# Layer-norm statistics of a two-layer diffusion step: variance, root and reciprocal on 128x3 token columns

## Chip, cores and metric

The kernel runs on one core of a Trainium2 chip. The time is that of one execution on the device, in microseconds. A core has TensorE (PE in the rows; PEld is its loading of weights), VectorE (DVE), ScalarE (ACT), GpSimd (POOL) and SyncE (SP), which issues transfers. Each works through its own list of instructions in order and waits on semaphores for the others.

## The reference

One step of a two-layer network over 384 tokens (128 context, 256 latent) of width 1024: layer 0 has an mLSTM and attention mixer and a dense SwiGLU, layer 1 a bidirectional Mamba-2 mixer and top-2-of-8 experts. Each of the four sub-layers ends in a layer norm, and these four norms are what the change touches:

```python
def layer_norm(x, g, b):
    xf = x.astype(jnp.float32)
    mu = xf.mean(-1, keepdims=True)
    var = jnp.mean(jnp.square(xf - mu), -1, keepdims=True)
    return ((xf - mu) * lax.rsqrt(var + EPS) * g + b).astype(x.dtype)

def post_norm_layer(x, mods, mixer, channel, ln):
    sh1, sc1, g1, sh2, sc2, g2 = mods
    y, state = mixer(x * (1 + sc1) + sh1)
    x = layer_norm(ALPHA * x + g1 * y, ln[0], ln[1])
    x = layer_norm(ALPHA * x + g2 * channel(x * (1 + sc2) + sh2), ln[2], ln[3])
    return x, state
```

All inputs are float32. The values of a token's norm are one mean and one variance over the 1024 features, so 384 of each.

## The kernel before

Activations lie with the features on the partitions: `zT[:, b, :]` is block b (of KB = 8) of 128 features by T = 384 tokens. A mean over features is therefore a sum over partitions and blocks. TensorE makes it with the matrix `onesm` (128x128, every entry 1/1024) as one operand and a block as the other: the result, in PSUM bank 6, has the mean of each of the 384 tokens, the same on all 128 partitions. The same with `sqT`, the squares from ScalarE (L740), gives the mean square in bank 7. A float32 product is two passes in the trace, so a product appears as x2 and a group of three as x6.

The norms are numbered ln = 0 to 3. In norm 0 (after the mixer's output products `mixo`) and norm 2 (after `ssdo`) six of the eight blocks are first added up on GpSimd (L588, L591; `SUMMED`), and TensorE takes the sum in one go (`sums`), with block 6 before it and block 7 behind. In norm 1 all eight blocks are taken one by one, block b-1 behind the down products of block b. In norm 3, the last, blocks 4 and 5, the sum of four, and a pair added up on VectorE are taken at the end. `after_block` sets these places. There is no scheduler: what stands in each engine's function is its order.

When mean (bank 6) and mean square (bank 7) are complete, the engines go on in `deviation` (ScalarE) and `norm_steps` (VectorE):

- ScalarE squares the mean (L748) and copies it to SBUF (L749), which GpSimd waits for to centre blocks 4 to 7 (L600).
- VectorE takes the difference of mean square and squared mean (L1366) and centres blocks 0 and 1 (L1361).
- ScalarE takes the root into `stdr` (L751).
- VectorE takes the reciprocal (L1371) and multiplies block by block (L1377), with the centring of blocks 2 and 3 and the low parts (`low`, L1671 in norm 0, L1735 in norm 1) between.
- ScalarE applies the modulation (L759) and writes the rounded high part (L891, L944); VectorE subtracts it for the low part; TensorE starts the next stage (L2527 in norms 0 and 1, L2820 in norm 2) with block 0's.

All of L748 to L1371 work on 128x384, with the same row on all partitions. Semaphores: `mean_mm` and `var_mm` from TensorE, `sq_ready` and `std_ready` from ScalarE, `dev_ready` and `norm_ready` from VectorE, `ax_ready` from GpSimd. `gss` and `gsd` are two small tiles of 128x3 that layer 1's gated norm uses too (L1042, L1894). In norm 2, ScalarE splits the first tile of expert weights (L1130) between the root and the modulation.

Of the kernel before, what the change touches and what calls it, by code (L numbers as in the profile page):

```python
# [16 lines left out]
ALU = mybir.AluOpType  # L17
ACT = mybir.ActivationFunctionType
X = mybir.AxisListType.X

P = 128
D = 1024
KB = D // P
TP, TS = 128, 256
T = TP + TS
C = T // P
# [72 lines left out]
def build(nc, i, o):  # L99
    ctx = ExitStack()  # L100
    with ctx:
# [24 lines left out]
        uT = placed("uT", [P, KB, T])  # L126
        zT = placed("zT", [P, KB, T])
        sqT = placed("sqT", [P, KB, T])
# [3 lines left out]
        onesm = sb("onesm", [P, P])  # L132
# [4 lines left out]
        ps = ctx.enter_context(nc.psum_tensor("ps", [P, 8, 512], F32))  # L137

        ident = cons[:, CI["ident"][0]:CI["ident"][1]]
# [102 lines left out]
        epsc = sm.take(1)  # L242
        hsq = qkr.rearrange("p c n -> p (c n)")[:, 0:HA * C * HD].rearrange("p (h c d) -> p h c d", h=HA, c=C)
        knew_v = wa.take(P)
        stdr = placed("stdr", [P, T])
        mean2, var, meanr = (uT[:, b, :] for b in (7, 6, 5))
        dsums = [uT[:, b, :] for b in (4, 4, 4, 0)]
        zpair = uT[:, 1, :]
        masks = stdr[:, 0:2 * P].rearrange("p (e t) -> p e t", e=2)
# [59 lines left out]
        gss = sm.take(C)  # L309
        gsd = sm.take(C)  # L310
# [86 lines left out]
        def S(name):  # L397
            if name not in sems:
                sems[name] = ctx.enter_context(nc.semaphore(name))
            return sems[name]  # L400
# [334 lines left out]
        def _(act):  # L735
            step = Serial(act, S("act_step"))
# [8 lines left out]

            def deviation(ln):
                act.wait_ge(S("mean_mm"), 2 * ln + 2)
                nc.scalar.activation(mean2, ps[:, 6, 0:T], ACT.Square).then_inc(S("sq_ready"), 1)  # L748
                nc.scalar.activation(meanr, ps[:, 6, 0:T], ACT.Copy).then_inc(S("sq_ready"), 1)  # L749
                act.wait_ge(S("dev_ready"), DEV * ln + KB + 2)  # L750
                nc.scalar.activation(stdr[:, :], var, ACT.Sqrt, bias=epsc).then_inc(S("std_ready"), 1)  # L751

            def modulated(layer, half, ln, b):

# [478 lines left out]
        def _(v):  # L1233
            step = Serial(v, S("dve_step"))
            V = nc.vector
# [123 lines left out]
            def norm_steps(ln, low=None):  # L1359
                def center(b):  # L1360
                    V.tensor_tensor(zT[:, b, :], zT[:, b, :], ps[:, 6, 0:T], ALU.subtract) \  # L1361
                        .then_inc(S("dev_ready"), 1)

                v.wait_ge(S("var_mm"), ln + 1)
                v.wait_ge(S("sq_ready"), (KB + 2) * ln + KB + 1)
                V.tensor_tensor(var, ps[:, 7, 0:T], mean2, ALU.subtract).then_inc(S("dev_ready"), 1)  # L1366
                v.wait_ge(S("sq_ready"), (KB + 2) * (ln + 1))
                center(0)
                center(1)
                v.wait_ge(S("std_ready"), ln + 1)  # L1370
                step(V.reciprocal(stdr[:, :], stdr[:, :]))  # L1371
                for b in range(KB):
                    if b < MID:
                        v.wait_ge(S("dev_ready"), DEV * ln + KB + b + 3)
                    else:
                        v.wait_ge(S("ax_ready"), ax_count(ln, "centered", b - MID + 1))
                    V.tensor_tensor(zT[:, b, :], zT[:, b, :], stdr[:, :], ALU.mult).then_inc(S("norm_ready"), 1)  # L1377
                    if b + 2 < MID:
                        center(b + 2)
                    if low and b >= 2:  # L1380
                        low(b - 2)
                if low:
                    low(KB - 2)
                    low(KB - 1)
# [56 lines left out]
            for e in range(2):  # L1441
                running_max(e, 0, 0.0)
                first, second = (1, 2) if e == 0 else (2, 1)
# [761 lines left out]
        def _(pe):  # L2205
            M = nc.tensor
# [21 lines left out]
            def first_mean(ln):  # L2228
# [2 lines left out]
                M.matmul(ps[:, MEAN_BANK[ln], 0:T], onesm[:, :], zT[:, 0, :], start=True, stop=True) \  # L2231
                    .then_inc(S("mean_mm"), 1)

            def moments(ln, *blocks):

                for b in blocks:
                    first = b == (0 if SUMMED[ln] == 0 else SUMMED[3] if ln == 3 else KB - 2)
                    last = ln < 3 and b == KB - 1
                    pe.wait_ge(S("dev_ready"), DEV * ln + b + 2)
                    m = M.matmul(ps[:, 6, 0:T], onesm[:, :], zT[:, b, :], start=first, stop=last)  # L2240
                    if last:
                        m.then_inc(S("mean_mm"), 1)
                    pe.wait_ge(S("sq_ready"), (KB + 2) * ln + b + 1)
                    m = M.matmul(ps[:, 7, 0:T], onesm[:, :], sqT[:, b, :], start=first, stop=last)
                    if last:
                        m.then_inc(S("var_mm"), 1)

            def sums(ln):

                pe.wait_ge(S("ax_ready"), ax_count(ln, "summed", 1))  # L2250
                M.matmul(ps[:, 6, 0:T], onesm[:, :], dsums[ln], start=False, stop=False)
                M.matmul(ps[:, 7, 0:T], onesm[:, :], sqT[:, 0, :], start=False, stop=False)

            def after_block(ln, b, first):

                if b == first:
                    first_mean(ln)
                elif SUMMED[ln] and b == KB - 1:
                    moments(ln, KB - 2)
                    sums(ln)  # L2260
                    moments(ln, KB - 1)
                elif not SUMMED[ln] and b > first:
                    moments(ln, *(range(b) if b == first + 1 else (b - 1,)))
                    if b == KB - 1:
                        moments(ln, b)

            pe.wait_ge(S("cact_ready"), 1)
            for t in range(ADA_PE):
# [7 lines left out]
            for k in range(KB):  # L2276
                pe.wait_ge(S("u_ready"), k + 1)
                m = M.matmul(ps[0:32, 2, 0:T], w[:, k * 32:(k + 1) * 32], uT[:, k, :], start=k == 0, stop=k == KB - 1)
# [16 lines left out]
            for t in range(3):  # L2295
                for part in range(4):
                    proj(t, part)
                    if (t, part) == (0, 1):
                        pe.wait_ge(S("gates_moved"), 1)
                        for n in range(2):  # L2300
                            m = M.matmul(ps[:, 6 + n, 0:T], con("spread", 32)[:, n * P:(n + 1) * P], gates32,
                                         start=True, stop=True)
                        m.then_inc(S("gate_mm"), 1)
            for j in range(4):
# [6 lines left out]
                for k in range(KB):  # L2311
                    c0 = k * 256 + (j % 2) * P
                    m = M.matmul(ps[:, 3 + j % 2, 0:T], slot(g % RING)[:, c0:c0 + P], uT[:, k, :],
                                 start=k == 0, stop=k == KB - 1)
# [4 lines left out]
            for c in range(C):  # L2319
                for j in range(4):  # L2320
                    m = M.transpose(ps[:, c, j * P:(j + 1) * P], qkr[:, c, j * P:(j + 1) * P], ident)
                m.then_inc(S("qkT_mm"), 1)
            for c, at in ((0, 0), (1, 2), (2, 3)):
                m = M.transpose(ps[:, 5, at * P:(at + 1) * P], qkr[:, c, 512:640], ident)
# [52 lines left out]
            for n in range(12):  # L2377
                q, c = n // C, n % C
                src = gli if q == 0 else rows[:, q - 1, :]
                m = M.transpose(ps[:, 5 + n // 4, (n % 4) * P:(n % 4 + 1) * P], src[:, c * P:(c + 1) * P], ident)  # L2380
            m.then_inc(S("cols_mm"), 1)
            for c in range(C):
                for j in range(4):
                    m = M.transpose(ps[:, c, j * P:(j + 1) * P], tokk[:, c, j * P:(j + 1) * P], ident)
# [583 lines left out]
            moments(3, 4, 5)  # L2968
            sums(3)
            pe.wait_ge(S("b16_ready"), 2)  # L2970
            M.matmul(ps[:, 6, 0:T], onesm[:, :], zpair, start=False, stop=True).then_inc(S("mean_mm"), 1)
            pe.wait_ge(S("b16_ready"), 3)
            M.matmul(ps[:, 7, 0:T], onesm[:, :], sqT[:, KB - 2, :], start=False, stop=True).then_inc(S("var_mm"), 1)

# [119 lines left out]
```

## Time and profile before

| | |
|---|---|
| median of 3 runs | 1596.39 us |
| lowest, highest | 1595.52, 1599.64 us |
| the profiled execution's own time | 1599.93 us |
| its span, first to last instruction | 1598.2 us |
| TensorE busy, mean granted clock | 94%, 0.977 |
| VectorE, ScalarE, GpSimd busy | 79%, 50%, 21% |
| end of the sums in norms 0, 1, 2, 3 | 299.6, 603.7, 970.5, 1585.3 us |

All times in the rows are microseconds from the start of the span. The granted clock is a share of 2.4 GHz: 1.00 or 0.50 (1.2 GHz). Matmuls are pipelined: one's duration runs from its start to its last result, and the next starts earlier. So the distance from start to start is what a product costs in a series, and the duration counts only for the last one.

### The profile page before, as it was taken

Reading aid. Unit: us, or ns where it says so; the run is one execution under the profiler, and the core shown is the slowest. Engines: PE = TensorE matmul, PEld = TensorE weight load, DVE = VectorE, ACT = ScalarE, POOL = GpSimd, SP = SyncE. Lnnn points to the kernel's source line nnn. Section 1 sums busy time; section 2 is a strip of 40 time slices with the busy share of each in tenths; the row PEclk is TensorE's granted clock in tenths of the full one; section 3 lists DMA queues with packets and bytes.
Section 4 is the critical chain, followed back from the end, with each engine's and each line's share of the span. In section 5 each row is a group of like instructions: output and inputs, shape, how many; then the busy total and the mean of one; then the engine's idle time right before and its main releaser. Section 6 shows DMA issues by size and latency. Waiting matters only on the chain. (4 is left out here: it accounts for less than half of the span.)

```text
span 1598.2 us, 23834 instructions
## 1 busy us (share of the span) xinstructions
PE 1498.7 (94%) x8783; PEld 1358.9 (85%) x8783; DVE 1262.1 (79%) x1668; ACT 801.2 (50%) x1069; POOL 332.4 (21%) x408
## 2 busy tenths in 40 slices
PE   4999999799999998999999897999999999999996
PEld 1768876599999997997776895999999999999995
DVE  6868789688887986886787745788888888888885
ACT  1222223533323227445677525567676776676763
POOL 2201003700000103002997053000011010110003
PEclk9999999899999998999999899999999999999998
DMA  9534344355566532233221036789999999999961
GB/s 379 188 112 167 132 134 154 103 214 216 198 239 237 214 119 105 106 106 132 93 80 67 1 142 257 265 307 367 365 376 359 346 366 361 384 347 347 366 258 40
DMA packets 50439, 349.68 MB, mean 219 GB/s; under 512 B 6048, under 2 KB 6448, under 8 KB 22720
## 3 DMA queue, kind: packets, MB, share of 16 engines
q1 hardware_dynamic: 31680, 278.88, 44.9%
q0 software_dynamic: 18256, 68.30, 12.7%
q10 hardware_dynamic: 432, 1.57, 0.2%
q8 instruction: 43, 0.70, 0.2%
q14 instruction: 28, 0.23, 0.0%
HBM read 335.22 MB, written 13.50 MB: 218 GB/s over the span
## 5 line engine op out<-in xcount | busy, mean ns | idle before, releaser
L2020 DVE TENSOR_TENSOR arena_r<-arena,arena_r 128x2816 fp32r<-128x2816 f32 x132 | 406.0, 3090 | 54.2 <-ACT arena_r L1130 52.8
L2892 PE MATMUL ps<-arena_r,uT_r 128*128 128x352 f32 (+1 forms) x1188 | 367.0, 309 | 0.0
L1130 ACT ACTIVATE arena_r<-arena 128x2816 fp32r<-128x2816 f32 x132 | 337.5, 2557 | 53.8 <-PE ps L2892 52.1
L2892 PE MATMUL ps<-arena_r,zT_r 128*128 128x352 f32 x1408 | 346.7, 327 | 5.3 <-DVE uT_r L2118 4.0
L2527 PE MATMUL ps<-sqT_r,arena_r 128*128 128x384 f32 x963 | 261.4, 343 | 7.5 <-DVE uT_r L1671 7.5
L2892 PEld LDWEIGHTS ps<-arena_r,zT_r 128*128 128x128 f32 x1408 | 247.3, 189 | 5.7 <-DVE arena_r L2020 5.7
L2892 PEld LDWEIGHTS ps<-arena_r,uT_r 128*128 128x128 f32 x1188 | 224.9, 189 | 0.0
L2527 PEld LDWEIGHTS ps<-sqT_r,arena_r 128*128 128x128 f32 x963 | 179.0, 191 | 8.2 <-issue 8.1
L2892 PE MATMUL ps<-arena_r,spare_r 128*128 128x256 f32 x968 | 177.8, 285 | 4.0 <-DVE arena_r L2020 4.0
L2527 PE MATMUL ps<-arena_r,arena_r 128*128 128x384 f32 x848 | 161.0, 343 | 5.8 <-DVE arena_r L1876 3.4
L2527 PEld LDWEIGHTS ps<-arena_r,arena_r 128*128 128x128 f32 x848 | 151.0, 192 | 8.3 <-DVE arena_r L1876 3.7
L2892 PEld LDWEIGHTS ps<-arena_r,spare_r 128*128 128x128 f32 x968 | 150.1, 190 | 6.3 <-DVE arena_r L2020 6.0
L2527 PE MATMUL ps<-uT_r,arena_r 128*128 128x384 f32 x448 | 152.9, 341 | 0.0
L2290 PE MATMUL ps<-arena,uT 128*128 128x256 f32 x432 | 99.5, 384 | 0.3 <-DVE small L1537 0.3
L2290 PEld LDWEIGHTS ps<-arena,uT 128*128 128x128 f32 x432 | 80.0, 190 | 16.2 <-issue 5.5
L1656 DVE TENSOR_TENSOR arena_r<-arena,arena_r 128x2048 fp32r<-128x2048 f32 (+1 forms) x30 | 76.3, 2544 | 16.5 <-ACT arena_r L878 16.3
L710 POOL DMA_INDIRECT y_rows<-sqT,rows_out x10 | 16.7, 1669 | 334.9 <-ACT sqT L1179 334.9
L2527 PEld LDWEIGHTS ps<-uT_r,arena_r 128*128 128x128 f32 x448 | 85.4, 191 | 0.0
L878 ACT ACTIVATE arena_r<-arena 128x2048 fp32r<-128x2048 f32 (+1 forms) x30 | 62.5, 2082 | 40.8 <-PE ps L2527 40.8
L701 POOL DMA_INDIRECT sqT<-u_rows,rows_in x10 | 37.6, 3763 | 144.8 <-DVE rows_in L2111 144.8
L905 ACT ACTIVATE zT<-ps 128x384 f32<-128x384 f32 x22 | 10.8, 492 | 110.0 <-PE ps L2527 110.0
L1069 ACT ACTIVATE arena<-ps,spare 128x128 f32<-128x128 f32 x192 | 53.2, 379 | 25.4 <-PE ps L2681 25.2
(468 smaller groups left out, 2469.5 us busy)
## 6 DMA issues: line engine op xcount, KB each, us to landing
arena<-in_w_moe SPq DMA_DIRECT2D x132, 1408.0 KB, 7.5
arena<-in_w_up SPq DMA_DIRECT2D x22, 1024.0 KB, 4.9
zT<-in_w_adav POOLq DMA_DIRECT2D x32, 512.0 KB, 4.7
arena<-in_w_xbc SPq DMA_DIRECT2D x12, 1024.0 KB, 4.9
arena<-in_w_down SPq DMA_DIRECT2D x8, 1408.0 KB, 6.4
spare<-in_w_adav POOLq DMA_DIRECT2D x20, 512.0 KB, 5.1
sqT<-in_w_adav POOLq DMA_DIRECT2D x16, 512.0 KB, 3.8
arena<-in_w_z SPq DMA_DIRECT2D x8, 1024.0 KB, 4.9
```

The lines of the kernel that those rows point to most:

```text
L701: gp.indirect_dma_start(xrow, None, u_dram, bass.IndirectOffsetOnAxis(ap=rows_in[:, :], axis=0)) \
L710: gp.indirect_dma_start(y_dram, bass.IndirectOffsetOnAxis(ap=rows_out[:, :], axis=0), ye, None, compute_op=ALU.add).then_inc(S("y_added"), 16)
L878: nc.scalar.activation(fwhi[n % 2][:, 0:width], slot(g % RING)[:, 0:width], ACT.Copy) \
L905: nc.scalar.activation(silu2[:, b, :], ps[:, 2 * b, 0:T], ACT.Silu).then_inc(S("silu_ready"), 1)
L1069: k = nc.scalar.activation(edec[:, h % 2, e, c * P:(c + 1) * P], ps[:, 3 + e, c * P:(c + 1) * P], ACT.Exp, bias=ncumc[:, 3 * e + c, h:h + 1])
L1130: nc.scalar.activation(whi[s % PAIRS], slot(s % MRING), ACT.Copy) \
L1656: V.tensor_tensor(slot_r(g % RING)[:, 0:width], slot(g % RING)[:, 0:width], fwhi[n % 2][:, 0:width].bitcast(F32), ALU.subtract).then_inc(S ...
L2020: V.tensor_tensor(wlo[s % PAIRS], slot(s % MRING), whi[s % PAIRS].bitcast(F32), ALU.subtract) \
L2290: m = M.matmul(ps[:, bank + c, 0:256], uT[:, k, c * P:(c + 1) * P], slot(g % RING)[:, k * 256:(k + 1) * 256], start=k == 0, stop=k == KB - 1)
L2527: m = M.matmul(out, a, b, start=first and n == 0, stop=last and n == 2)
L2892: m = M.matmul(out, a, b, start=first and n == 0, stop=last and n == 2)
```

## The change

The wide product for the mean of a block stays. Beside it `mean_part` makes three narrow ones: here the block is the stationary operand, 128 tokens at a time, and one column of `onesm` is the moving one. The result is one column per 128 tokens, with token t on partition t: the mean as 128x3, in bank 6 beside the wide one. For the squares `square_part` makes only the three narrow products, and the wide one is gone. Squared mean, difference, root and reciprocal then work on 128x3 (`gss`, `gsd`). `inverse_rows` brings the result back to 128x384: for each of the three columns one product with the column, repeated 128 times, as the stationary operand and the identity as the moving one, into bank 7. VectorE multiplies with bank 7 in place of `stdr`. `std_ready` and `var_mm` now count twice per norm.

```diff
@@ deviation (ScalarE)
-                nc.scalar.activation(mean2, ps[:, 6, 0:T], ACT.Square).then_inc(S("sq_ready"), 1)
+                nc.scalar.activation(gss, ps[:, 6, T:T + C], ACT.Square).then_inc(S("sq_ready"), 1)
                 nc.scalar.activation(meanr, ps[:, 6, 0:T], ACT.Copy).then_inc(S("sq_ready"), 1)
                 act.wait_ge(S("dev_ready"), DEV * ln + KB + 2)
-                nc.scalar.activation(stdr[:, :], var, ACT.Sqrt, bias=epsc).then_inc(S("std_ready"), 1)
+                nc.scalar.activation(gsd, gsd, ACT.Sqrt, bias=epsc).then_inc(S("std_ready"), 1)
@@ norm_steps (VectorE)
-                v.wait_ge(S("var_mm"), ln + 1)
+                v.wait_ge(S("var_mm"), 2 * ln + 1)
                 v.wait_ge(S("sq_ready"), (KB + 2) * ln + KB + 1)
-                V.tensor_tensor(var, ps[:, 7, 0:T], mean2, ALU.subtract).then_inc(S("dev_ready"), 1)
+                V.tensor_tensor(gsd, ps[:, 7, 0:C], gss, ALU.subtract).then_inc(S("dev_ready"), 1)
                 v.wait_ge(S("sq_ready"), (KB + 2) * (ln + 1))
                 center(0)
+                v.wait_ge(S("std_ready"), 2 * ln + 1)
+                V.reciprocal(gsd, gsd).then_inc(S("std_ready"), 1)
                 center(1)
-                v.wait_ge(S("std_ready"), ln + 1)
-                step(V.reciprocal(stdr[:, :], stdr[:, :]))
+                v.wait_ge(S("var_mm"), 2 * ln + 2)
...
-                    V.tensor_tensor(zT[:, b, :], zT[:, b, :], stdr[:, :], ALU.mult).then_inc(S("norm_ready"), 1)
+                    V.tensor_tensor(zT[:, b, :], zT[:, b, :], ps[:, 7, 0:T], ALU.mult).then_inc(S("norm_ready"), 1)
@@ TensorE
+            def mean_part(z, first, last):
+
+                M.matmul(ps[:, 6, 0:T], onesm[:, :], z, start=first, stop=False)
+                for c in range(C):
+                    m = M.matmul(ps[:, 6, T + c:T + c + 1], z[:, c * P:(c + 1) * P], onesm[:, 0:1], start=False,
+                                 stop=last and c == C - 1)
+                if last:
+                    m.then_inc(S("mean_mm"), 1)
+
+            def square_part(sq, first, last):
+
+                for c in range(C):
+                    m = M.matmul(ps[:, 7, c:c + 1], sq[:, c * P:(c + 1) * P], onesm[:, 0:1], start=first and c == 0,
+                                 stop=last and c == C - 1)
+                if last:
+                    m.then_inc(S("var_mm"), 1)
+
+            def inverse_rows(ln):
+
+                pe.wait_ge(S("std_ready"), 2 * ln + 2)
+                for c in range(C):
+                    m = M.matmul(ps[:, 7, c * P:(c + 1) * P], gsd[:, c:c + 1].broadcast_to([P, P]), ident,
+                                 start=True, stop=True)
+                m.then_inc(S("var_mm"), 1)
```

`moments`, `sums` and the end of norm 3 call `mean_part` and `square_part` where they had the wide products, and `inverse_rows` stands behind the last of them in each norm.

The order on TensorE at norm 1, from the last down product (L2527) over blocks 6 and 7 to the next stage; before:

```order
L2527 MATMUL ps<-arena_r_53,arena_r_51 128x384
L2240 MATMUL ps<-zT,onesm 128x384
L2244 MATMUL ps<-sqT,onesm 128x384
L2240 MATMUL ps<-zT,onesm 128x384
L2244 MATMUL ps<-sqT,onesm 128x384
L2527 MATMUL ps<-sqT_r_62,spare_r_57 128x384
```

and of the changed kernel, where that product is L2551:

```order
L2551 MATMUL ps<-arena_r_53,arena_r_51 128x384
L2237 MATMUL ps<-zT,onesm 128x384
L2239 MATMUL ps<-onesm,zT 128x1 x3
L2247 MATMUL ps<-onesm,sqT 128x1 x3
L2237 MATMUL ps<-zT,onesm 128x384
L2239 MATMUL ps<-onesm,zT 128x1 x3
L2247 MATMUL ps<-onesm,sqT 128x1 x3
L2256 MATMUL ps<-cons,small 128x128 x3
L2551 MATMUL ps<-sqT_r_62,spare_r_57 128x384
```

Behind each wide product stand three narrow ones more, the wide products of squares have become three narrow ones each, and the three with the identity (L2256) come ahead of the next stage.

VectorE at norm 1, from the difference to the first low part; before:

```order
L1366 TENSOR_TENSOR uT<-ps,uT 128x384
L1361 TENSOR_TENSOR zT<-zT,ps 128x384 x2
L1371 RECIPROCAL stdr<-stdr 128x384
L1377 TENSOR_TENSOR zT<-zT,stdr 128x384
L1361 TENSOR_TENSOR zT<-zT,ps 128x384
L1377 TENSOR_TENSOR zT<-zT,stdr 128x384
L1361 TENSOR_TENSOR zT<-zT,ps 128x384
L1377 TENSOR_TENSOR zT<-zT,stdr 128x384
L1735 TENSOR_TENSOR uT_r_49<-uT,sqT_r_62 128x384
```

and of the changed kernel:

```order
L1366 TENSOR_TENSOR small<-ps,small 128x3
L1361 TENSOR_TENSOR zT<-zT,ps 128x384
L1370 RECIPROCAL small<-small 128x3
L1361 TENSOR_TENSOR zT<-zT,ps 128x384
L1378 TENSOR_TENSOR zT<-zT,ps 128x384
L1361 TENSOR_TENSOR zT<-zT,ps 128x384
L1378 TENSOR_TENSOR zT<-zT,ps 128x384
L1361 TENSOR_TENSOR zT<-zT,ps 128x384
L1378 TENSOR_TENSOR zT<-zT,ps 128x384
L1736 TENSOR_TENSOR uT_r_49<-uT,sqT_r_62 128x384
```

The centring of block 1 now stands behind the reciprocal, and the products (L1378) read `ps` where they read `stdr`.

## Rows read from the trace of the kernel before

**Rows 1.** The page's first part: busy time of each engine over the span
```profile
PE 1498.7 (94%) x8783; PEld 1358.9 (85%) x8783; DVE 1262.1 (79%) x1668; ACT 801.2 (50%) x1069; POOL 332.4 (21%) x408
```

**Rows 2.** Busy time per stretch; columns PE, PEld, DVE, ACT, POOL, clock, DMA share, GB/s
```profile
307.00:600.00 293.00, 290.46 (x1608) 286.71 (x1609) 237.34 (x312) 96.83 (x103) 32.66 (x54) 0.98 0.54 199
...
1000.00:1572.00 572.00, 560.17 (x3864) 553.52 (x3865) 479.04 (x374) 387.38 (x252) 58.09 (x25) 0.99 0.87 336
```

**Rows 3.** Timeline of norm 1: start, duration, engine, line, operation, idle before and its releaser
```profile
602.12 0.91 PE L2240 MATMUL ps<-zT,onesm 128*128 128x384 f32 x2 [0.27 <-DVE zT L1344]
...
603.71 0.56 DVE L1366 TENSOR_TENSOR uT<-ps,uT 128x384 f32<-128x384 f32 x1 [1.65 <-PE ps L2244]
...
604.18 1.01 DVE L1361 TENSOR_TENSOR zT<-zT,ps 128x384 f32<-128x384 f32 x2
...
605.11 2.55 DVE L1371 RECIPROCAL stdr<-stdr 128x384 f32<-128x384 f32 x1
607.69 0.61 DVE L1377 TENSOR_TENSOR zT<-zT,stdr 128x384 f32<-128x384 f32 x1
...
610.56 0.55 DVE L1735 TENSOR_TENSOR uT_r<-uT,sqT_r 128x384 fp32r<-128x384 f32 x1
...
611.25 0.66 PE L2527 MATMUL ps<-sqT_r,spare_r 128*128 128x384 f32 x1 [7.58 <-DVE uT_r L1735]
```

**Rows 4.** Timeline of norm 0, same columns
```profile
295.07 1.24 PE L2251 MATMUL ps<-uT,onesm 128*128 128x384 f32 x2 [2.33 <-POOL sqT L591]
...
297.38 1.49 PE L2240 MATMUL ps<-zT,onesm 128*128 128x384 f32 x2
...
299.64 0.56 DVE L1366 TENSOR_TENSOR uT<-ps,uT 128x384 f32<-128x384 f32 x1 [6.85 <-PE ps L2244]
...
307.14 0.66 PE L2527 MATMUL ps<-sqT_r,arena_r 128*128 128x384 f32 x1 [7.53 <-DVE uT_r L1671]
```

**Rows 5.** Timeline of norm 2, same columns
```profile
970.46 0.56 DVE L1366 TENSOR_TENSOR uT<-ps,uT 128x384 f32<-128x384 f32 x1 [3.00 <-PE ps L2244]
...
971.58 2.54 ACT L1130 ACTIVATE arena_r<-arena 128x2816 fp32r<-128x2816 f32 x1
...
975.09 0.99 ACT L759 ACTIVATE uT<-zT,mods 128x128 f32<-128x128 f32 x2 [0.98 <-DVE zT L1377]
```

**Rows 6.** Chain that ended last, norm 3: start, duration, what
```profile
1575.22 0.67 PE ps L2883 x6
...
1579.83 0.65 PE ps L2240 x2
1580.48 0.88 PE ps L2244 x2
```

**Rows 7.** Timeline of TensorE, narrow products: latest first
```profile
1007.24 0.82 PE L2867 MATMUL ps<-spare,zT 128*128 128x10 f32 x6
1007.91 0.57 PE L2892 MATMUL ps<-arena_r,zT_r 128*128 128x352 f32 x2
...
984.86 0.35 PE L2824 MATMUL ps<-cons,spare 8*128 8x8 f32 x3 [0.71 <-DVE spare L2026]
...
883.27 1.54 PE L2693 MATMUL ps<-arena 128*128 128x64 f32 x6
```

**Rows 8.** 128x3 operations by line: shortest/median/longest in ns
```profile
L1042 ACT ACTIVATE small<-small x4: 300/302/303, 807.9 to 903.2; 128x3 f32<-128x3 f32 x4
...
L1894 DVE RECIPROCAL small<-small x2: 170/174/178, 894.3 to 903.6; 128x3 f32<-128x3 f32 x2
```

**Rows 9.** Busy time and granted clock of short stretches, columns as in Rows 2
```profile
307.10:312.50 5.40, 5.36 (x17) 5.39 (x18) 5.19 (x9) 5.27 (x13) 5.40 (x5) 0.50 0.00 0
...
611.20:616.30 5.10, 5.05 (x16) 5.08 (x17) 4.88 (x8) 5.00 (x12) 5.10 (x5) 0.50 0.01 3
...
1579.50:1585.70 6.20, 5.73 (x19) 2.94 (x18) 3.10 (x5) 2.64 (x6) 2.17 (x4) 1.00 0.00 0
876.00:889.00 13.00, 12.06 (x42) 9.41 (x42) 11.14 (x19) 10.86 (x32) 0.00 (x0) 0.50 0.00 1
```

More of the change, by code:

```diff
@@ L245, in build @@
         stdr = placed("stdr", [P, T])
-        mean2, var, meanr = (uT[:, b, :] for b in (7, 6, 5))
+        meanr = uT[:, 5, :]
         dsums = [uT[:, b, :] for b in (4, 4, 4, 0)]
@@ L2239, in moments @@
                     pe.wait_ge(S("dev_ready"), DEV * ln + b + 2)
-                    m = M.matmul(ps[:, 6, 0:T], onesm[:, :], zT[:, b, :], start=first, stop=last)
-                    if last:
-                        m.then_inc(S("mean_mm"), 1)
+                    mean_part(zT[:, b, :], first, last)
                     pe.wait_ge(S("sq_ready"), (KB + 2) * ln + b + 1)
-                    m = M.matmul(ps[:, 7, 0:T], onesm[:, :], sqT[:, b, :], start=first, stop=last)
-                    if last:
-                        m.then_inc(S("var_mm"), 1)
+                    square_part(sqT[:, b, :], first, last)
             def sums(ln):
                 pe.wait_ge(S("ax_ready"), ax_count(ln, "summed", 1))
-                M.matmul(ps[:, 6, 0:T], onesm[:, :], dsums[ln], start=False, stop=False)
-                M.matmul(ps[:, 7, 0:T], onesm[:, :], sqT[:, 0, :], start=False, stop=False)
+                mean_part(dsums[ln], False, False)
+                square_part(sqT[:, 0, :], False, False)
             def after_block(ln, b, first):
@@ L2261, in after_block @@
                     moments(ln, KB - 1)
+                    inverse_rows(ln)
                 elif not SUMMED[ln] and b > first:
@@ L2265, in after_block @@
                         moments(ln, b)
+                        inverse_rows(ln)
             pe.wait_ge(S("cact_ready"), 1)
@@ L2970, in _ @@
             pe.wait_ge(S("b16_ready"), 2)
-            M.matmul(ps[:, 6, 0:T], onesm[:, :], zpair, start=False, stop=True).then_inc(S("mean_mm"), 1)
+            mean_part(zpair, False, True)
             pe.wait_ge(S("b16_ready"), 3)
-            M.matmul(ps[:, 7, 0:T], onesm[:, :], sqT[:, KB - 2, :], start=False, stop=True).then_inc(S("var_mm"), 1)
+            square_part(sqT[:, KB - 2, :], False, True)
+            inverse_rows(3)
 def blocks(w, n):
```

## The prediction

> **What bounds the kernel now.** I read the page's busy shares first: TensorE is busy for 94% of the span, VectorE for 79%, ScalarE for 50% [rows 1]. The table by stretches then shows where the missing 6% lie: between the norms TensorE is busy for 290.5 of 293 us and for 560 of 572 us [rows 2]. So a microsecond that TensorE gains or loses at a norm reaches the end, and work of the other engines between the norms is covered. What is left are the four norms. In the timeline of norm 1 the reader sees three pieces. The last sum of squares ends where the difference (L1366) starts, at 603.71. From there to the first product with the inverse root (L1377 at 607.69) it takes 3.98 us, 2.55 of them the reciprocal over 384 columns. From L1377 to the first product of the next stage (L2527 at 611.25) it takes 3.56 more, through ScalarE and the first low part (L1735 at 610.56) [rows 3]. TensorE idles 7.58 us for it. Norm 0 has the same shape, from 299.64 to 307.14 [rows 4].
>
> **What one norm's sums cost.** A wide product with the ones matrix (two passes over 384 columns) takes 0.65 us [rows 6]. Its narrow replacement is three products of two passes each, with a data block of 128x128 as weights and one moving column. The nearest rows have 10 moving columns and the same weights: six passes from 1007.24 to 1007.91, 0.67 us, or 0.11 us a pass [rows 7]; six passes with 128 moving columns take 0.67 us too [rows 6]. That 10 and 128 columns cost the same says that the weights set the pace, so I take 0.67 us for one column. Three narrow products thus cost as much as one wide product of 384 columns. A mean block keeps its wide product and gains three narrow ones: +0.67. A square block swaps one for the other: +0.02. A block costs 0.69 us more.
>
> Norm 0. Block 6 lies before the wait for GpSimd (2.33 us idle [rows 4]), which hides its 0.69. The sums and block 7 lie behind it: 2 x 0.69 = 1.4, and since the first of them run at half clock (the pair at 297.38 lasts 1.49 where norm 1 shows 0.91 [rows 3, 4]), I take 1.5.
> Norm 1. Blocks 0 to 5 are summed between the down products, where TensorE is the bound: 6 x 0.69 = 4.2. Blocks 6 and 7 add 1.4, less the 0.27 us that TensorE waits for block 7 now [rows 3]: 1.1.
> Norm 2. Block 6, the sums and block 7, all on the path: 3 x 0.69 = 2.1.
> Norm 3. Blocks 4 and 5, the sums and the pair: 4 x 0.69 = 2.8, less the 0.23 us by which the squares wait for ScalarE now (0.88 against 0.65 [rows 6]): 2.5.
> Added: 1.5 + 5.3 + 2.1 + 2.5 = 11.4 us. This is the dear part of the edit.
>
> **What the tail of a norm gives back.** Between the last narrow product and L1377's first product stand now: the difference on 128x3, 0.17 (priced as the reciprocal of that size, L1894); the root on 128x3, 0.30 (L1042) [rows 8]; the reciprocal on 128x3, 0.17; three products with the identity, 0.67 plus some 0.16 until the last has drained; four handovers of some 0.04 (L1371 ends 0.03 before L1377 starts [rows 3]). That is 1.63. The centring of block 0 (0.54: L1361 has two in 1.01 [rows 3]) stands between difference and reciprocal on VectorE and outlasts the root by about 0.12: 1.8 us in place of 3.98, a gain of 2.2. At half clock the six passes take twice as long and drain later: 2.5, a gain of 1.5. The new wait of VectorE for the root has behind it only the reciprocal and the centring of block 1; that one, now behind the reciprocal, is hidden beside the identity products. GpSimd's centring waits for the copied mean, which ScalarE starts earlier after a square of 128x3.
>
> Norm 0: between the two, 1.85. Norm 1: 2.2. Norm 3: 2.2. Norm 2 is held by another: ScalarE splits a weight tile (L1130, 2.54 us from 971.58) between the root and the first modulated block at 975.09 [rows 5]. The split can't shrink. Counted from the start of the difference (L1366 at 970.46), it starts after 1.12 us now and the modulated block after 4.63; then the split would start after some 0.5 (0.17 and 0.30) and end after 3.05, while the first product with the inverse is done by 2.4. So ScalarE decides, 3.05 in place of 4.63: 1.6.
> Given back: 1.85 + 2.2 + 1.6 + 2.2 = 7.85 us.
>
> **The products with the inverse.** They read it from PSUM now instead of from SBUF. In norm 1 five VectorE operations lie between 607.69 and L1735 at 610.56, 2.87 us, or 0.57 each, while L1361, which reads PSUM, is followed by its like after 0.47 [rows 3], beside a busy GpSimd too. Five at 0.47 are 2.35: 0.5 us earlier for the first low part in norms 0 and 1, 1.0 together. In norms 2 and 3 ScalarE paces this piece, so nothing there.
> The Trainium skill, "SBUF — State Buffer", section "Who interferes with whom", says that a VectorE instruction with two SBUF inputs contends with a GpSimd one that reads SBUF, and one with at most one SBUF input does not. Without that effect the sum would be 1.0 us higher. The rows agree so far as they go, since only the PSUM form keeps its 0.47.
>
> **The clock.** After the norms TensorE works at 0.50 for about 5.4 and 5.1 us [rows 9], 2.6 us of loss each. The change breaks TensorE's idle time of 7.6 us into about 1 and 3.1 us, with 0.7 of work between. The longer half could still bring the clock down, so I count nothing here and keep 0 to 5 us gained as a rival.
>
> **The sum.** 11.4 - 7.85 - 1.0 = +2.6 us. The profiled execution took 1599.93 us (span 1598.2, and 1.7 around it), so it becomes 1602.5. The median of the three runs is 1596.39, and by the same difference 1599.0.
>
> **The rivals.**
> First, the clock falls among the narrow sums. Against: norm 3's sums stand at 1.00 now [rows 9]. For: from 876 to 889 the clock was 0.50 for 13 us though TensorE was busy for 12.06 of them [rows 9], with products of 64 columns among them; a busy engine is no warrant for the clock, and one column is far less. Place: norms 2 and 3 and the piece after them. Price: norm 3's eight groups and four wide products are some 8 us; if the later 4 us of them ran at half clock they took 4 more; norm 2, with 6 us, 2 more; the identity products 0.7 each, in two norms. About +7, so 1606.0, slower by 0.6%. It decides once some 2.2 us of such loss come on top of my +2.6.
> Second, weights in a slower rhythm. If a pass with one column cost 0.15 in place of 0.11, 34 groups of six passes would add 8 us: 1607. No row shows it; slower too.
> Third, the clock stays up after norms 0 and 1. Then the loss of 2.6 us in each falls away, 5.2 together: 1593.8. Faster by 0.16%, below what can be told. For: the idle time is cut in two. Against: 3.1 us of idle is left.
> Fourth, narrow products are cheaper than the rows. The three with 8 moving columns and one pass each follow in 0.07 us (0.35 for three, less the last's 0.2) [rows 7]. At 0.07 a pass 34 groups cost 14.3 instead of 22.8, 8.5 less: 1590.5, faster by 0.4%.
> The Trainium skill, "TensorE: Matmul & The Clock Gate", section "Back-to-back issue gap", gives about 60 cycles, 25 ns, for 1 to 64 columns without the weight load. An estimate by it is 34 x 6 x 0.025 = 5.1 us for all groups, and a kernel some 15 us faster than before. The rows with 10 and 64 columns speak against it, as their weights change with every pass; it is part of the fourth rival.
> That the change doesn't do what it says can't be: the order shows the reciprocal on 3 columns.
>
> **How the numbers follow.** About 0.3%, 4.8 us, is what a measurement of this kernel can tell: below 1591.6 is faster, above 1601.2 slower. The forecast, with its own range of 1596 to 1602.5 (0.64 to 0.72 for a group is 2 us; tails within 0.3 each): 0.55. First rival 0.14, second 0.08, third 0.15, fourth 0.08. Faster: the fourth and a little of the third, 0.10. Slower: the first, the second and the upper edge of the forecast, 0.27. Same: 0.63. The range of 1593 to 1606.5 leaves out the fourth and a tenth above.
>
> **What would show it.** Right: the six narrow passes in 0.67; L1378's first product about 1.8 us after L1366 starts in norms 1 and 3; RECIPROCAL at 0.17; in norm 2 ScalarE's first modulated block straight behind its split; the down stage longer by 4.2. Wrong: a granted clock below 1 in the stretches of sums (first rival); L1378 at 0.7 beside GpSimd; narrow groups under 0.5; the clock at 1.00 when TensorE resumes after norms 0 and 1 (third).

## The result

| | kernel before | changed kernel |
|---|---|---|
| median of 11 runs each | 1597.70 us | 1605.13 us |
| lowest, highest | 1594.34, 1601.75 us | 1600.04, 1606.96 us |
| ratio to before, 95% interval | | 1.0042 (1.0029 to 1.0054) |
| profiled execution, its span | 1599.93, 1598.2 us | 1600.04, 1598.3 us |
| its mean granted clock | 0.977 | 0.973 |

The change makes the kernel slower by 0.42%, 6.7 us. The profiled execution of the changed kernel is the fastest of its eleven and that of before lies above its median, so the two spans are equal and their difference says little. What they do show is each norm in detail. The first part of the page of the changed kernel, to be held against [rows 1]:

```profile
PE 1515.4 (95%) x8987; PEld 1381.2 (86%) x8987; DVE 1249.2 (78%) x1668; ACT 796.9 (50%) x1069; POOL 325.5 (20%) x408
```

TensorE is busy for 16.7 us more, VectorE for 13 less. Not all of that is the change's own: ahead of norm 0, where nothing was changed, the clock of this execution falls twice for 3.4 us (at 38 and 103 us), which that of the one before does not, and block 6 of norm 0 comes at 292.39 and not at 291.29. The stretches between the norms, and three shorter ones within the sums (same columns as [rows 2]):

```profile
307.00:608.00 301.00, 296.21 (x1699) 293.44 (x1700) 240.40 (x322) 99.55 (x111) 31.77 (x57) 0.98 0.55 197
...
999.40:1559.00 559.60, 548.33 (x3785) 542.94 (x3785) 473.49 (x364) 384.44 (x249) 56.49 (x23) 0.99 0.89 344
298.00:302.60 4.60, 4.60 (x18) 3.98 (x18) 0.00 (x0) 0.55 (x2) 0.54 (x1) 0.50 0.00 0
1577.90:1584.30 6.40, 6.40 (x45) 5.43 (x44) 2.62 (x4) 1.76 (x4) 1.72 (x2) 1.00 0.00 0
1584.50:1587.00 2.50, 2.41 (x13) 2.32 (x11) 0.00 (x0) 0.55 (x2) 0.70 (x1) 0.50 0.00 0
```

Between the norms TensorE is as full as before (of the 4.8 us that the first row leaves free, 1.2 lie before its first product at 308.19). How fast its products follow one another there is not the same in the two profiles; that comes up under the price of the sums below. In norm 1 the work runs as forecast; the timeline answers to [rows 3]:

```profile
602.97 0.81 PE L2237 MATMUL ps<-zT,onesm 128*128 128x384 f32 x2
...
603.61 0.72 PE L2239 MATMUL ps<-onesm,zT 128*128 128x1 f32 x6
...
604.20 0.81 PE L2247 MATMUL ps<-onesm,sqT 128*128 128x1 f32 x6
...
604.87 0.89 PE L2237 MATMUL ps<-zT,onesm 128*128 128x384 f32 x2
...
605.60 0.72 PE L2239 MATMUL ps<-onesm,zT 128*128 128x1 f32 x6
...
606.18 0.81 PE L2247 MATMUL ps<-onesm,sqT 128*128 128x1 f32 x6
...
607.03 0.16 DVE L1366 TENSOR_TENSOR small<-ps,small 128x3 f32<-128x3 f32 x1 [2.40 <-PE ps L2247]
...
607.57 0.17 DVE L1370 RECIPROCAL small<-small 128x3 f32<-128x3 f32 x1
...
607.79 1.31 PE L2256 MATMUL ps<-cons,small 128*128 128x128 f32 x6 [0.80 <-DVE small L1370]
609.14 0.55 DVE L1378 TENSOR_TENSOR zT<-zT,ps 128x384 f32<-128x384 f32 x1 [0.96 <-PE ps L2256]
...
611.47 0.55 DVE L1736 TENSOR_TENSOR uT_r<-uT,sqT_r 128x384 fp32r<-128x384 f32 x1
...
612.16 0.66 PE L2551 MATMUL ps<-sqT_r,spare_r 128*128 128x384 f32 x1 [3.06 <-DVE uT_r L1736]
```

A narrow group of means takes 0.59 from its start to the squares' start (603.61 to 604.20), one of squares 0.67. The difference and the reciprocal take 0.16 and 0.17 us where they took 0.56 and 2.55. From the difference to the first product with the inverse it is 2.11 us, where 3.98 stood; from there to the next stage 3.02, where 3.56 stood. TensorE's idle time of 7.58 us is down to 0.80 and 3.06. In norm 2 the prediction named ScalarE's split (L1130); it runs from 971.19, and the modulated blocks (L759) follow it without a gap, where [rows 5] had nearly 1 us between the two:

```profile
971.19 2.53 ACT L1130 ACTIVATE arena_r<-arena 128x2816 fp32r<-128x2816 f32 x1
973.63 7.11 ACT L759 ACTIVATE uT<-zT,mods 128x128 f32<-128x128 f32 x16
```

In norm 3 something else is to be seen. The end of its chain (start, duration, what), the piece that [rows 6] showed before the change:

```profile
1582.56 0.56 PE ps L2239 x6
1583.12 0.67 PE ps L2247 x6
1583.79 0.76 PE ps L2237 x2
1584.56 1.07 PE ps L2239 x6
1585.63 1.29 PE ps L2247 x6
...
1587.00 0.16 DVE small L1366
...
1587.77 1.66 PE ps L2256 x6
1589.46 0.55 DVE zT L1378
```

A group of means takes 0.56, the next one 1.07; a group of squares 0.67, then 1.29; the products with the identity 1.66, where the timeline has 0.93 in norm 2, at full clock. Between them, at 1584.4, the granted clock goes from 1.00 to 0.50, as the two rows of stretches above show (1577.90 and 1584.50). Before the fall TensorE was busy in all 6.40 us of its stretch. No idle time precedes it. In norm 0 the clock falls too, behind the wait for GpSimd as it did before, but there it rose again at 298.9, while the last product of squares ran (from 298.66), and now the sums run at 0.50 to their end (298.00 to 302.60), with TensorE busy throughout.

| from the profiled executions, us | before | changed | changed, second profile | `e4_more_columns` |
|---|---|---|---|---|
| norm 0, block 6's product to the difference | 8.35 | 10.32 | 11.66 | 7.80 |
| norm 2, the same | 4.07 | 6.04 | 7.94 | 6.15 |
| norm 3, block 4's product to the difference | 5.65 | 9.22 | 9.60 | 8.20 |
| difference to first product with the inverse, norms 0, 2, 3 | 3.98, 3.98, 3.98 | 2.45, 1.74, 2.46 | 2.45, 2.45, 2.44 | 1.74, 1.74, 1.74 |

### The profile page after: what moved, and what is told of

The parts are those of the page before. It is cut to its first block and busy times, and to the rows that moved or that the text cites. A ratio compares the mean times of both kernels' runs of the same rounds, so it can differ in the third digit from the quotient of the medians.

```text
span 1598.3 us, 24242 instructions
## 1 busy us (share of the span) xinstructions
PE 1515.4 (95%) x8987; PEld 1381.2 (86%) x8987; DVE 1249.2 (78%) x1668; ACT 796.9 (50%) x1069; POOL 325.5 (20%) x408
## 5 line engine op out<-in xcount | busy, mean ns | idle before, releaser
L1130 ACT ACTIVATE arena_r<-arena 128x2816 fp32r<-128x2816 f32 x132 | 337.4, 2556 | 53.8 <-PE ps L2916 52.1
L2551 PE MATMUL ps<-sqT_r,arena_r 128*128 128x384 f32 x963 | 256.8, 338 | 3.1 <-DVE uT_r L1672 3.1
L2551 PEld LDWEIGHTS ps<-sqT_r,arena_r 128*128 128x128 f32 x963 | 176.0, 189 | 3.4 <-issue 3.3
L2551 PE MATMUL ps<-arena_r,arena_r 128*128 128x384 f32 x848 | 161.5, 344 | 6.2 <-DVE arena_r L1877 3.4
L2551 PEld LDWEIGHTS ps<-arena_r,arena_r 128*128 128x128 f32 x848 | 152.3, 194 | 7.3 <-DVE arena_r L1877 3.7
L2551 PE MATMUL ps<-uT_r,arena_r 128*128 128x384 f32 x448 | 150.9, 337 | 0.0
L710 POOL DMA_INDIRECT y_rows<-sqT,rows_out x10 | 16.7, 1674 | 335.3 <-ACT sqT L1179 335.3
L2551 PEld LDWEIGHTS ps<-uT_r,arena_r 128*128 128x128 f32 x448 | 84.6, 189 | 0.0
L547 POOL DMA_DIRECT2D zT<-in_w_adav x32 | 17.0, 530 | 230.9 <-DVE arena L1240 126.1
```

Source lines behind the costliest of these rows:

```text
L547: gp.dma_start(adaw[layer][b] if dst is None else dst, src[n] if isinstance(n, int) else src[ds(n, 1)].rearrange("a p n -> (a p) n")).then ...
L710: gp.indirect_dma_start(y_dram, bass.IndirectOffsetOnAxis(ap=rows_out[:, :], axis=0), ye, None, compute_op=ALU.add).then_inc(S("y_added"), 16)
L1130: nc.scalar.activation(whi[s % PAIRS], slot(s % MRING), ACT.Copy) \
L2551: m = M.matmul(out, a, b, start=first and n == 0, stop=last and n == 2)
```

## The experiments

Two theories for what the sum of +2.6 us lacks. **Clock**: TensorE's granted clock falls within the narrow sums, because a pass with one moving column is hardly any work for the array, however busy TensorE counts as. **Price**: groups or handovers cost more than the rows said, at any clock. All times below stand against runs of the kernel before on the same chip (29 runs in the first set of four, 23 in the second set of three); the clock is the median over the runs of each run's mean granted clock, stretches in which TensorE idles included.

| | ratio to before, 95% interval | in us | mean clock |
|---|---|---|---|
| before | 1 | 0 | 0.976 |
| `e0_after` | 1.0044 (1.0030 to 1.0058) | +7.0 | 0.970 |
| `e4_more_columns` | 1.0013 (1.0003 to 1.0023) | +2.1 | 0.9805 |
| `e3_means_only` | 1.0059 (1.0041 to 1.0076) | +9.4 | 0.9745 |
| `e1_mean_once` | 0.9979 (0.9967 to 0.9991) | -3.4 | 0.974 |
| `e2_norm1` | 1.0017 (1.0005 to 1.0029) | +2.7 | 0.976 |
| `e5_norms023` | 1.0047 (1.0029 to 1.0064) | +7.5 | 0.971 |
| `e6_once_columns` | 0.9966 (0.9954 to 0.9977) | -5.4 | 0.9785 |

### e0_after: the changed kernel again

> The changed kernel again, beside the others of this call. It is the yardstick on this chip for the clock shares. Both theories expect about 1.0042 of the kernel before, +6.7 us. My sum from rows gives +2.6; what is above it is open. Theory A (clock): the extra comes from TensorE's granted clock, which falls in the narrow sums and with them the identity products: the runs above +5 us should show a mean clock of 0.970 or lower, those near +2.6 us one near 0.974, and the kernel before 0.976 or so. Theory B (price): the narrow groups or handovers cost more than 0.67 us; then the time should be above the sum at an equal clock too.

Measured: 1604.47 us, ratio 1.0044, the first result again. The time follows the clock from run to run: the four runs with a mean clock of 0.973 or 0.974 took 1599.3 to 1601.8 us, the eight with 0.967 to 0.971 took 1604.1 to 1609.9. The first four lie around 1600.0, which is this chip's median before, 1597.4, and the sum's 2.6; that speaks for the clock theory. In the eleven runs of the result time and clock go together less closely (correlation -0.56, here -0.81). The profile shows the fall in norm 0, again behind the wait for GpSimd, and within the sums of norms 2 and 3 (stretches, columns as in [rows 2]):

```profile
968.60:972.30 3.70, 3.70 (x29) 3.17 (x27) 0.84 (x2) 0.52 (x1) 0.00 (x0) 1.00 0.71 241
972.50:976.40 3.90, 3.90 (x15) 3.23 (x14) 0.00 (x0) 0.55 (x2) 0.59 (x1) 0.50 1.03 439
...
1584.00:1590.00 6.00, 6.00 (x44) 5.21 (x44) 2.61 (x4) 1.76 (x4) 1.76 (x2) 1.00 0.00 0
1590.30:1593.40 3.10, 3.10 (x14) 2.74 (x12) 0.00 (x0) 0.55 (x2) 0.58 (x1) 0.50 0.00 0
```

In both norms TensorE is busy in the whole stretch ahead of the fall, 3.70 of 3.70 and 6.00 of 6.00 us, at 1.00; and behind it at 0.50. The timeline of TensorE in norm 2 shows what that does to a group:

```profile
969.16 0.72 PE L2239 MATMUL ps<-onesm,zT 128*128 128x1 f32 x6
969.75 0.81 PE L2247 MATMUL ps<-onesm,sqT 128*128 128x1 f32 x6
...
973.87 1.28 PE L2239 MATMUL ps<-onesm,zT 128*128 128x1 f32 x6
975.01 1.42 PE L2247 MATMUL ps<-onesm,sqT 128*128 128x1 f32 x6
```

The means start at 969.16 and 0.59 us later the squares; at 973.87, 1.14 us later.

### e4_more_columns: more moving columns, equal passes

```diff
-                    m = M.matmul(ps[:, 6, T + c:T + c + 1], z[:, c * P:(c + 1) * P], onesm[:, 0:1], start=False,
+                    m = M.matmul(ps[:, 6, T + 42 * c:T + 42 * c + 42], z[:, c * P:(c + 1) * P], onesm[:, 0:42], start=False,
...
-                    m = M.matmul(ps[:, 7, c:c + 1], sq[:, c * P:(c + 1) * P], onesm[:, 0:1], start=first and c == 0,
+                    m = M.matmul(ps[:, 7, 128 * c:128 * (c + 1)], sq[:, c * P:(c + 1) * P], onesm[:, 0:128], start=first and c == 0,
```

(ScalarE and VectorE read the first column of each group.)

> The changed kernel, with more moving columns in the narrow products, at an equal number of passes and weight loads: 42 columns for the means and 128 for the squares in place of 1. Only the first of each group is read. In the rows of before, passes with 10 and with 128 columns both take 0.11 us, so the sums should not get longer. Theory A (the clock falls because a pass with one column is hardly any work for the array): the clock stays up in more of the stretches of sums, mean clock 0.002 to 0.003 above e0_after's, and 2 to 4 us faster than it. Theory B (price of passes and handovers, clock without part in it): within 1 us of e0_after.

Measured: 1.0013, 4.9 us faster than the changed kernel, with a mean clock of 0.9805 instead of 0.970. More work for the array at the same number of passes makes the kernel faster. The sums did not get longer: at full clock a block with its two narrow groups takes 1.98 us from one wide product to the next in norm 3 of either kernel (1576.36 to 1578.34 here, 1579.69 to 1581.67 in the changed one). Timeline of norm 0:

```profile
299.05 0.76 PE L2239 MATMUL ps<-onesm,zT 128*128 128x42 f32 x6
...
299.63 0.92 PE L2247 MATMUL ps<-onesm,sqT 128*128 128x128 f32 x6
...
300.58 0.16 DVE L1366 TENSOR_TENSOR small<-ps,small 128x3 f32<-128x3 f32 x1 [4.39 <-PE ps L2247]
...
302.32 0.55 DVE L1378 TENSOR_TENSOR zT<-zT,ps 128x384 f32<-128x384 f32 x1 [0.58 <-PE ps L2256]
```

From means to squares it is 0.58 us, and the tail from 300.58 to 302.32 is 1.74 us. The stretches of sums in norms 2 and 3 run at full clock to their end:

```profile
961.70:967.70 6.00, 6.00 (x43) 5.07 (x41) 0.83 (x2) 1.08 (x3) 0.02 (x1) 1.00 0.81 304
1574.40:1582.50 8.10, 8.07 (x58) 6.82 (x56) 2.63 (x4) 2.32 (x6) 1.92 (x3) 1.00 0.00 0
```

The price theory had expected less than 1 us. What is left, +2.1 us, lies near the sum's +2.6, but is no clean check of it, since the mean clock here also stands above that of the kernel before (0.9805 and 0.976). The cleaner check are the sums of norms 2 and 3 themselves, at 1.00 in both kernels: 6.15 and 8.20 us in place of 4.07 and 5.65 (last table of the result), so 2.1 and 2.55 more, where 2.1 and 2.5 were forecast.

### e3_means_only: the narrow means without the tail

Shown against the kernel before, shortened:

```diff
 def mean_part(ln, z, first, last):
+                for c in range(C):
+                    m = M.matmul(ps[:, 6, T + c:T + c + 1], z[:, c * P:(c + 1) * P], onesm[:, 0:1], start=False, ...
```

> The kernel before with the changed kernel's narrow mean products alone, their results unused; squares, root, reciprocal and products with the inverse as before. 17 groups on the path (one more in norm 0 is covered). The forecast's price of 0.67 us a group gives 11.4 us, less 0.5 that waits hide: +10.9 us over before. If the clock falls in them too, +12 to +15. If a group costs 1.0 us and more: +16 and above. If the forecast's fourth rival held (0.42 a group): +7.

Measured: +9.4 us (6.5 to 12.1). With the 0.5 us that waits hide, 17 groups cost 9.9, 0.58 each. Chain of norm 2:

```profile
972.44 0.65 PE ps L2252 x2
973.08 0.56 PE ps L2254 x6
973.64 0.77 PE ps L2262 x2
```

A group takes 0.56 us and the wide product behind it 0.12 more than the 0.65 of one behind another wide one; together 0.68, which the prediction took as 0.67. The clock here, 0.9745, is only a little under before's: between two groups of means two wide products, of squares and of the next mean, still stand. The fourth rival (0.42 a group, +7) lies within the interval, but the rows of the chain rule it out.

### e2_norm1 and e5_norms023: by place

```diff
+        COLS = (1,)          # in e5_norms023: (0, 2, 3)
...
+                if ln in COLS:
+                    nc.scalar.activation(gss, ps[:, 6, T:T + C], ACT.Square).then_inc(S("sq_ready"), 1)
+                else:
+                    nc.scalar.activation(mean2, ps[:, 6, 0:T], ACT.Square).then_inc(S("sq_ready"), 1)
```

(and so for each changed line).

> The change in norm 1 alone; norms 0, 2 and 3 as before. The forecast's terms for it: +5.3 for the eight blocks, -2.2 for the tail, -0.5 for the products with the inverse: +2.6 us. The clock theory adds little here, since only blocks 6 and 7 stand together and the others lie among wide down products: ratio 1.001 to 1.0025, mean clock within 0.001 of before. If it is nearer to +5 us, norm 1 carries what the forecast missed.

> The change in norms 0, 2 and 3, norm 1 as before: the complement. The forecast's terms: norm 0 -0.85, norm 2 +0.5, norm 3 +0.3, 0.0 us together. The clock theory puts the missing 4 to 5 us here, where the groups of all blocks stand in a row: +3 to +5 us (ratio 1.002 to 1.003), mean clock 0.003 to 0.005 below before. Price theory: the missing part is spread by the number of groups (4, 6 and 8 here, 16 in norm 1), so half of it, +2.

Measured: norm 1 alone +2.7 us (0.8 to 4.6) with an unchanged clock of 0.976, where the prediction's terms give +2.6. Norms 0, 2 and 3 together: +7.5 us (4.6 to 10.2) with a clock of 0.971, where they give 0.0. So what the sum missed lies, as far as these intervals tell, in these three, where the groups of all blocks stand in a row, and not in norm 1, which has half of all groups but has them among down products. The profile of `e5_norms023` has the fall in all three: at 0.50 TensorE is busy for 7.30 of 7.30 us in norm 0 (from 293.8), 2.87 of 2.90 in norm 2 (from 969.5) and 3.59 of 3.60 in norm 3 (from 1583.9), each up to the difference. The size came out above both expectations; the interval is wide (six runs), and only its lower end, 4.6, lies in the +3 to +5 of the clock theory. The price theory's +2 lies outside.

### e1_mean_once: the means once per norm

```diff
-                nc.scalar.activation(gss, ps[:, 6, T:T + C], ACT.Square).then_inc(S("sq_ready"), 1)
...
                 nc.scalar.activation(meanr, ps[:, 6, 0:T], ACT.Copy).then_inc(S("sq_ready"), 1)
+                act.wait_ge(S("mean_mm"), 3 * ln + 3)
+                nc.scalar.activation(gss, ps[:, 6, T:T + C], ACT.Square, scale=float(KB)).then_inc(S("std_ready"), 1)
...
+            def mean_columns(ln):
+
+                pe.wait_ge(S("sq_ready"), (KB + 1) * (ln + 1))
+                for c in range(C):
+                    m = M.matmul(ps[:, 6, T + c:T + c + 1], meanr[:, c * P:(c + 1) * P], onesm[:, 0:1], start=True,
+                                 stop=True)
+                m.then_inc(S("mean_mm"), 1)
```

(the narrow products in `mean_part` are gone).

> The changed kernel, with the narrow mean products once per norm in place of once per block: the mean that ScalarE copies to SBUF is the same on all partitions, and three narrow products of this copy with the column of 1/1024, times 8 in ScalarE's square, give the mean on 128x3. Removes 18 groups and adds 4. By my sum: 17 groups on the path of 0.68 us go (11.5 us); in each norm the tail grows by the copy (0.5), the group (0.57 to 0.67) and two handovers, less the 0.67 us in which the last squares run beside the copy: about 0.8 each, 3.2 in all. So 8 us faster than the changed kernel, and about 1.5 us or more faster than before (ratio 0.996 to 1.000), with more if the clock falls less often in shorter sums (theory A: mean clock at least 0.001 above e0_after). Theory B with dearer groups expects a gain above 12 us over the changed kernel.

Measured: 0.9979, 3.4 us faster than before and 10.4 faster than the changed kernel. The removed groups account for 8.3 of that by the working on record; the clock rose from 0.970 to 0.974 as well, and the rest of 2 us is of a size with it.

### e6_once_columns: both

The means as in `e1_mean_once`, and the narrow products of the squares with 128 moving columns:

```diff
-                    m = M.matmul(ps[:, 7, c:c + 1], sq[:, c * P:(c + 1) * P], onesm[:, 0:1], start=first and c == 0,
+                    m = M.matmul(ps[:, 7, c * P:(c + 1) * P], sq[:, c * P:(c + 1) * P], onesm[:, :], start=first and c == 0,
```

> Both single edits together on the changed kernel: the mean columns once per norm (e1) and 128 moving columns in the narrow products of the squares (e4). If the clock theory is right, the gain of the second comes on top of the first, since e1's mean clock of 0.974 still lies under e4's 0.9805: mean clock 0.980 or more, 2.5 to 4.5 us faster than e1, so 6 to 8 us faster than before (ratio 0.995 to 0.9965). Rival: what e4 gained came from its narrow mean products alone, which e1 no longer has; then e6 stays within 1 us of e1 (0.998) with a mean clock of 0.974 to 0.976.

Measured: 1590.78 us, 0.9966: 5.4 us faster than before, and the fastest of all. It is 2 us faster than `e1_mean_once` by the two ratios (intervals of 0.9954 to 0.9977 and 0.9967 to 0.9991, which overlap), less than the 2.5 to 4.5 expected; the clock is 0.9785, 0.0015 short of the number on record. The rival on record (within 1 us of `e1_mean_once`, clock 0.974 to 0.976) fits less well, but the overlap doesn't exclude it. Its norm 2 (timeline):

```profile
962.91 0.81 PE L2237 MATMUL ps<-zT,onesm 128*128 128x384 f32 x2
...
963.56 0.83 PE L2252 MATMUL ps<-onesm,sqT 128*128 128x128 f32 x6
963.76 0.49 ACT L748 ACTIVATE uT<-ps 128x384 f32<-128x384 f32 x1 [1.85 <-PE ps L2237]
...
964.30 0.83 PE L2245 MATMUL ps<-onesm,uT 128*128 128x1 f32 x6
...
965.17 0.17 ACT L750 ACTIVATE small<-ps 128x3 f32<-128x3 f32 x1 [0.92 <-PE ps L2245]
965.45 0.16 DVE L1367 TENSOR_TENSOR small<-ps,small 128x3 f32<-128x3 f32 x1 [4.09 <-ACT small L750]
...
967.18 0.55 DVE L1378 TENSOR_TENSOR zT<-zT,ps 128x384 f32<-128x384 f32 x1 [0.59 <-PE ps L2262]
```

The copy of the mean (L748) runs beside the last squares. The one group of means (L2245) starts at 964.30. The last squares have drained at 964.39 (963.56 and 0.83) and the difference starts at 965.45: the detour costs 1.06 us in a norm, where 0.8 was on record. The tail is 1.73 us.

## Why the prediction was right, and where not

The measured 1605.13 us lies in the range of 1593 to 1606.5, near its upper end, and the likeliest value of 1599.0 was 6 us too low. On the ratio the change costs 6.7 us where +2.6 was forecast; 1.3 us of the distance is only that the median before was 1597.7 in eleven runs and 1596.39 in three. By the prediction's own bounds the outcome is "slower", which had 0.27, and not "same", which had 0.63. Its own range ended at 1602.5; that the stated one holds the result is owed to the first rival, whose 1606.0 set the upper edge.

**What bounds the kernel**: right. Between the norms TensorE is as full as before and the time moves with it.

**The price of the sums**: right. 0.67 us for a group is 0.56 to 0.59 for means and 0.67 for squares, plus 0.1 for the wide product behind. The term by which the down products of norm 1 get longer, 4.2 us for six blocks, is best read from the profile of `e2_norm1`, whose clock falls in this stage at the same places as before's, to 0.3 us: from the first product behind norm 0 to block 6 of norm 1 it takes 297.19 us (307.14 to 604.33), the kernel before 293.26 (307.14 to 600.40), so 3.9 more. In the profile of the changed kernel the stage is only 1.5 us longer than before (308.19 to 602.97). Part of that is the clock: it is at half for 2.4 us less behind norm 0, which gives 1.2 back, and at half for 3.4 us more within the stage, which takes up to 1.7. The rest is something that the prediction did not have: products that the change doesn't touch follow one another faster. Three of them take 0.53 us from start to start before and 0.52 after; in the same 150 us, at full clock and with TensorE busy throughout, stand 851 and 867 of them (columns: length, busy TensorE, clock, DMA share, GB/s; before, then changed):

```profile
330.00:480.00 150.00, 150.00 (x851) 1.00 0.59 219
...
330.00:480.00 150.00, 150.00 (x867) 1.00 0.61 224
```

That is 1.9%; over the 193 us from 307 to 500 an estimate by it is 3.6 us. The profiles of before, `e2_norm1` and `e5_norms023` have 851 there, the other six 867 or 868. With one profile of most kernels it can't be told whether this belongs to the kernel or to the execution, and what sets it is not shown.

**The tail**: right in its pieces. 1.8 us at full clock was 1.74, and 2.5 at half clock 2.45; only norm 3's, forecast at full clock, ran at half. In norm 2 ScalarE decides, 2.94 us after the difference (970.79 to 973.73 in the chain) against 3.05 forecast.

**The products from PSUM**: right. L1378 takes 0.55 us in all 32 cases, beside a busy GpSimd too, and the first low part comes 2.33 us after the first product (609.14 to 611.47), forecast 2.35. The rule of the Trainium skill that was cited ("SBUF — State Buffer", "Who interferes with whom") agrees with that; by the trace it is worth the 0.5 us in each of two norms.

**The clock**: this is the step that failed. "I count nothing here", the prediction says, and it looked at the pieces after the norms only; the fall within the sums was its first rival, with 0.14. The rival was right in place (norm 3 and norm 2, and also norm 0), and in cause. In size it was too large by half: 1606.0 is 7.0 over the forecast's time, where 4.1 (6.7 less 2.6, with whatever else the sum lacks) and 4.9 (the gain of `e4_more_columns`) were measured. Over all nine profiles the place fits: of the sums of norms 2 and 3, five of six were cut by a fall where the change stands as it is (the changed kernel twice, and `e5_norms023`), one of two in `e1_mean_once`, 0.4 us before its end, none of four with more columns (`e4_more_columns`, `e6_once_columns`), and none of six with wide products between (before, `e2_norm1`, `e3_means_only`). The row from 876 to 889 [rows 9] had shown it: busy for 12.06 of 13 us at 0.50. It deserved the larger chance, since the change makes just that kind of work out of half of each sum. What argued against it, norm 3's sums at 1.00 [rows 9], was a row of wide products, so of other work than the one forecast.

**The third rival**, that the clock stays up after the norms, did not come as such: in the changed profile it is at 0.50 when TensorE resumes after norms 0 and 1, though for 3.0 and 2.8 us (to 311.2 and 615.0) in place of 5.4 and 5.1. In this profile that is 2.3 us less lost, where the prediction counted nothing. **The second** is refuted by 0.11 us a pass, **the fourth** by the same rows. With it falls the estimate from the Trainium skill ("TensorE: Matmul & The Clock Gate", "Back-to-back issue gap"), 25 ns for a narrow pass. That figure is for passes without a weight load; here each pass has its own, and 0.09 to 0.11 us a pass were measured with one column.

What stays open: at which share of narrow work the clock falls. It falls in some executions and not in others (time and clock scatter together in `e0_after`), and no experiment here was made to find the bound. In norm 0 the time from block 6 to the difference varied by 1.3 us between two profiles of the same kernel. Open too is why the two halves, 2.7 us for `e2_norm1` and 7.5 for `e5_norms023`, add up to 10.2 where the whole costs 6.7 to 7.0. The intervals allow it. So would the pace of the products between norms 0 and 1, if it belongs to the kernel: both halves and before have the slower one, and the whole would get some 3.6 us back by the faster. Its own cost would then be larger by that than the sum and the clock have been given here.

## What to carry to other kernels

Price a product by its weights as well as by its columns: three passes of one column after three loads of 128x128 cost as much as one wide product, so a reduction into columns pays once per result and not once per summand. Where a value is already the same on all partitions, three products of it with a column turn it, once, at the end. And when small products replace large ones on TensorE, look at the granted clock and not at the busy share: giving each pass more columns than it needs cost no time here and gave back 4.9 us.

## What was not expected of the hardware

TensorE's granted clock fell from 1.00 to 0.50 in stretches in which it was busy without a gap (6.00 of 6.00 us in norm 3, 3.70 of 3.70 in norm 2), with wide products of 384 columns and two groups of one-column products in turn. With 42 and 128 columns in the same passes it stayed at 1.00 in the same places (8.07 of 8.10 us busy) of the one profiled execution, and the median of the mean clocks over twelve runs rose from 0.970 to 0.9805. With one column it doesn't fall each time: the sums of norm 2 stayed at 1.00 in one of the two profiles. The busy share in a profile doesn't tell the two apart.

Equal products also had two paces at the same granted clock: 851 or 867 of them in the same 150 us, at 1.00 and with TensorE busy throughout. What sets the pace is not shown.
